# Placing the split expert activations phi and plo at another address of SBUF

## The reference, cut

```
def _peer(xn, w_query, sub_keys, expert_down, expert_up):
    ...
        u = expert_down[idx]
        v = expert_up[idx]
        act = jax.nn.gelu(jnp.einsum("td,thkd->thk", xb, u).astype(jnp.float32), approximate=False)
        return jnp.einsum("thk,thkd->td", (gate * act).astype(v.dtype), v)
...
def second_block(...):
    ...
        h = rmsnorm(x, ffn_norm[i])
        u = causal_dwconv(h @ w_up[i], conv_w[i], conv_b[i])
        x = x + (jax.nn.gelu(u) * (h @ w_gate[i])) @ w_down[i]
        g = jax.nn.sigmoid(rmsnorm(x, ple_norm[i]) @ w_ple_gate[i])
        x = x + (p[i] @ w_ple[i]) * g
    return rmsnorm(x, final_norm)
```

## Time and profile before

| | |
|---|---|
| median of 3 runs | 1329.02 us |
| the profiled execution's span | 1327.4 us |
| TensorE busy | 1310.4 us, 99% of the span |
| VectorE busy | 943.1 us, 71% |
| ScalarE busy | 725.3 us, 55% |
| mean DMA rate | 191 GB/s |

### The profile page before, as it was taken

How to read it: one execution, slowest core, us unless ns; L and a number is a source line. 1 busy time by engine, 2 the same in 40 slices (tenths; PEclk the granted TensorE clock), 3 DMA queues, 4 the chain that set the end, 5 groups by cost and what they waited for, 6 DMA issues and landing times. The chain is left out here.

```text
span 1327.4 us, 26387 instructions
## 1 busy us (share of the span) xinstructions
PE 1310.4 (99%) x8853; PEld 1196.9 (90%) x8853; DVE 943.1 (71%) x1766; ACT 725.3 (55%) x1077; POOL 517.7 (39%) x276
## 2 busy tenths in 40 slices
PE   8999999999999999999999999999999999999997
PEld 8999899999999999998888888788789888999986
DVE  6885677999998467766666666666666667676665
ACT  6833557777777743344444444444465446444446
POOL 1010002888887888787787778100000000000000
PEclk9999999999999999999999999999999999999999
DMA  7459554777767766668777778777674335555551
GB/s 257 149 194 383 197 175 154 180 185 184 183 177 186 191 168 153 142 146 216 209 208 211 213 213 209 262 234 228 213 242 162 112 115 183 181 188 183 184 191 64
DMA packets 119325, 253.03 MB, mean 191 GB/s; under 512 B 44336, under 2 KB 60848, under 8 KB 118752
## 3 DMA queue, kind: packets, MB, share of 16 engines
q1 hardware_dynamic: 77232, 229.24, 53.5%
q0 software_dynamic: 42032, 22.99, 10.9%
HBM read 234.23 MB, written 17.96 MB: 190 GB/s over the span
## 5 line engine op out<-in xcount | busy, mean ns | idle before, releaser
L456 DVE TENSOR_TENSOR wlo<-raw,whi 128x1024 fp32r<-128x1024 f32 x412 | 503.1, 1223 | 156.3 <-ACT whi L443 147.5
L443 ACT ACTIVATE whi<-raw 128x1024 fp32r<-128x1024 f32 x412 | 435.1, 1058 | 305.8 <-PE ps L462 292.8
L409 POOL DMA_INDIRECT gates_dense<-gate,spot x256 | 506.1, 1977 | 170.2 <-issue 78.7
L460 PE MATMUL ps<-ahi,whi 128*128 128x256 f32 x1824 | 522.5, 286 | 2.9 <-DVE alo L537 2.6
L461 PE MATMUL ps<-alo,whi 128*128 128x256 f32 x1824 | 515.9, 283 | 0.0
L462 PE MATMUL ps<-ahi,wlo 128*128 128x256 f32 x1824 | 515.7, 283 | 0.0
L460 PEld LDWEIGHTS ps<-ahi,whi 128*128 128x128 f32 x1824 | 349.9, 192 | 7.5 <-issue 5.8
L461 PEld LDWEIGHTS ps<-alo,whi 128*128 128x128 f32 x1824 | 349.4, 192 | 0.9
L462 PEld LDWEIGHTS ps<-ahi,wlo 128*128 128x128 f32 x1824 | 349.4, 192 | 0.0
L460 PE MATMUL ps<-whi,phi 128*128 128x512 f32 x600 | 238.2, 397 | 1.2 <-DVE plo L1854 1.1
L462 PE MATMUL ps<-whi,plo 128*128 128x512 f32 x600 | 237.8, 396 | 0.0
(11 more groups left out here) (367 smaller groups left out, 1088.0 us busy)
## 6 DMA issues: line engine op xcount, KB each, us to landing
raw<-in_wts SPq DMA_DIRECT2D x412, 512.0 KB, 3.7
gates_dense<-pf POOLq DMA_DIRECT2D x4, 4096.0 KB, 30.8
gd<-gates_dense SPq DMA_DIRECT2D x22, 256.0 KB, 4.8
gd<-gates_dense SPq DMA_DIRECT2D x10, 512.0 KB, 5.8
gates_dense<-gate,spot POOLq DMA_INDIRECT x256
cst<-in_c POOLq DMA_DIRECT2D x1, 1216.0 KB, 6.5
xt<-in_x_tok SPq DMA_DIRECT2D x2, 512.0 KB, 4.5
kk<-in_keys POOLq DMA_DIRECT2D x1, 1024.0 KB, 5.2
```

The source lines that it names most:

```text
L409: pl.indirect_dma_start(out=dense, out_offset=bass.IndirectOffsetOnAxis(ap=spot[:, tb, h, k:k + 1], axis=0), in_=gate[:, tb, h, k:k + 1], ...
L443: nc.scalar.activation(whi[:, j, :], raw_tile(j // 2, j % 2), ACT.Copy).then_inc(s["w_hi"], 1)
L456: nc.vector.tensor_tensor(wlo[:, j, :], raw_tile(j // 2, j % 2), whi[:, j, :].bitcast(F32), ALU.subtract).then_inc(s["w_lo"], 1)
L460: nc.tensor.matmul(out_ap, wh, xh, start=first, stop=False, skip_group_check=True)
```

## The change

`phi` and `plo` are placed directly behind `ones`, ahead of `vec`. They then start at 83072 and 85120, multiples of 64 (and of 128). `oh2` and `oheq` move with them, to the same two addresses. `vec`, `warm`, `wm`, `xt`, `pf` and what is cut out of `xt` and `pf` move up by 4096 bytes, and keep their remainder by 64. `ea` stays at 98272, and so does all that is cut out of it. No instruction is added, removed or moved; only addresses differ.

```diff
         ident = place("ident", [P])
         ones = place("ones", [P])
+        parts = top[0]
+        phi = place("phi", [2, T], F32R)
+        plo = place("plo", [2, T], F32R)
+        parts_end = top[0]
         vec = place("vec", [N_CV])
         warm = place("warm", [8])
         wm = place("wm", [KT])
...
         pf = place("pf", [2, T])
         aux_end = top[0]
-        phi = place("phi", [2, T], F32R)
-        plo = place("plo", [2, T], F32R)
         aux = [small]
...
-        aux = [aux_end]
+        aux = [parts]
         oh2 = place("oh2", [2, P, GT], F16, at=aux)
         oheq = place("oheq", [2, SPLIT, GT], F16, at=aux)
-        assert aux[0] <= top[0]
+        assert aux[0] <= parts_end
```

## The result

| | before | after |
|---|---|---|
| median of 8 runs | 1329.23 us | 1333.03 us (1332.05 to 1334.34) |
| span of the profiled execution | 1327.4 us | 1331.9 us |
| forecast | | 1315.7 us (1313.0 to 1322.5) |

The ratio is 1.003, with a 95% interval of 1.0021 to 1.0039. The forecast had a gain of 1.0%.

What follows compares the result with a forecast made beforehand. TensorE's step from matmul to matmul was taken as the bound. Up-projection 11.8 + feed-forward network 1.5 + oh2 0 = 13.3 us less, from 1329.0 to 1315.7 us, range 1313.0 to 1322.5.

Steps and rivals of the forecast that it cites:

- What bounds the kernel: Whole kernel: TensorE is busy 1310.4 of 1327.4 us, so only a shorter step between matmuls can save time.
- The step goes from 234.4 to 226.6 ns: Matmuls with phi or plo stationary: starting at a multiple of 64 bytes brings ahi's step, 7.8 ns less each.
- The up-projection gains 11.8 us: Up-projection: 1536 matmuls with phi or plo at 7.8 ns less, 12.0 us, taken as 11.8.
- The feed-forward network gains 1.5 us: Feed-forward network: 22 runs of 12 matmuls go from 2.81 to 2.72-2.75 us, saving 1.3 to 2.0, taken as 1.5.
- oh2 at 0: 256 small float16 matmuls with oh2 stationary: no change taken, with 2.0 us to either side as bound.
- pthi as control: Matmuls with pthi stationary, which the change doesn't touch: their step stays at 233.5 ns.
- What is late next: Feeders of the shorter up-projection tile: plo's slack of 0.80 us loses 0.09; the wait at the last tile grows 0.05.
- I would be wrong if TensorE showed new idle time in the up-projection: The prediction's own test for the changed kernel's profile; its other failure sign was a lower step without a shorter stage.
- Slower: 1335 us: Rival, chance 0.04: writers of phi and plo, in one bank with TensorE's reads, hold these up; 5.9 us lost.
- Place has no part: Rival, chance 0.11: something else phi and pthi share, such as stationary-to-moving distance, sets the step; 1329 us.

Runs made afterwards that it cites:

- Both edits of the scatters: Kernel before, once with the last 16 of 256 scatters left out (ratio 0.9998), once with VectorE's wlo split into two 512-column instructions (0.9999).
- rem0: Kernel before with wm placed behind plo, so phi starts at 94144, a multiple of 64 but not of 128; 1327.14 us.
- new64: Changed kernel with warm and wm ahead of phi, so phi starts at 83136, 64 bytes behind a multiple of 128; whi and wlo stay; 1328.01 us.
- all64: Changed kernel with every buffer from raw to plo moved up by 64 bytes, warm and wm folded into vec; 1333.98 us.

## Point by point: where the prediction was right, and where it failed

- **What bounds the kernel** (TensorE's step): right for the kernel before. Both edits of the scatters moved it by nothing (0.9998, 0.9999).
- **The step goes from 234.4 to 226.6 ns**: right in number, 226.67, and lucky in its cause. A multiple of 64 isn't what makes it (`rem0`, `new64`: 233.3). The address that the change happened to give, 83072, lies at `ahi`'s distance from `whi`, 0 modulo 512 bytes.
- **The up-projection gains 11.8 us**: right in kind, 11.3 in size. Matmul by matmul, TensorE was 7.6 us ahead of the kernel before at 838.82, and won 3.7 on the rest.
- **The feed-forward network gains 1.5 us**: mis-sized, 1.0. A run of 12 went from 2.80 to 2.75, at the upper end of the 2.72 to 2.75; but the 48 narrower matmuls behind it went from 5.745 to 5.752 us, which the sum had at nothing.
- **oh2 at 0**: right. Its matmuls keep a step of 81.8 ns in both.
- **pthi as control**: right. Six steps in 1.40 us (1102.40 to 1103.80 in the kernel after), as in the earlier trace rows; 1.40 / 6 is 233.3 ns, not the 233.5 of the prediction. It controlled for the chip, not for the cause: pthi is slow at its own distance.
- **What is late next**: this step failed, and with it the sign: it put the cost of a shorter tile at nothing. It asked of ScalarE, VectorE, and the DMA rate, at a place in the middle of the stage, and never of GpSimd and of SyncE's wait for it. The cost was a stall of 14.1 us and 2.6 us at the lower clock, 16.7 against 11.3 + 1.0 won: 4.4 us. Measured were 4.5 between the spans.
- **"I would be wrong if TensorE showed new idle time in the up-projection"**: it did, and that was the case. But the prediction gave no mechanism for it and no chance, and had 0.85 for a faster kernel.
- **The rivals.** "Slower: 1335 us" came near the measured time for a wrong reason: it had the writers of phi and plo hold up the reads, and with an average step of 226.67 over 1008 matmuls there is no room for that. "Place has no part" is refuted by `new64` against the kernel after. Its argument, a distance between the stationary and the moving operand, was set aside because phi and pthi share a level; by `all64` it was the better description.

In the trace of the kernel before, three rows could have shown it: the last scatter at 831.82, SyncE's one wait of 3.9 us for a scatter ahead of 837.82, and ScalarE's one wait of 2.19 us for a DMA where all its neighbours have 1.45 for TensorE. One question would have led there: which queue has a wait, once in this stage, that doesn't move with TensorE?

## What to carry to other kernels

Before a bound is made shorter, look for the one-time joins behind it (a wait in a DMA queue, a tail of another engine's work) and read their slack at their own place, not in the middle of the stage; a releaser that changes for one instruction is the mark of a join without slack. Work of GpSimd can be locked to VectorE's rhythm, so its pace has to be read again when the rhythm changes; splitting the long VectorE instruction freed it here for 0.06 us. And an address that helps is to be measured, and protected in the code, since 64 bytes took the gain away.

## What the runs showed of the hardware that was not expected

- With the place of the stationary operand, the step of a fp32r matmul of 512 columns went between 226.6 and 234.4 ns. Stationary and moving operand moved together by 64 bytes: 226.6 (`all64`). The stationary one alone by 64: 233.3 (`new64`). The 256-wide ones with ahi moving stayed near 120.
- An indirect DMA's issue on GpSimd took 1.54 us alone, and 2.42 to 2.54 us when it started 0.22 to 0.10 us behind a VectorE instruction of 1.22 us with two SBUF inputs. The VectorE instruction was hardly held by a scatter that had started with it or before it: 1.22 to 1.28 us.
- A stream of scatters got slower (2.55 to 2.64 us each in the mean, 2.50 to 2.72 where undisturbed) when the tile became 0.09 us shorter.
- After 14 us of idle time TensorE's granted clock was 0.50, and it was back at 1.00 in the window from 859 us, some 6 us of work later; that cost 2.6 us.
